# HGRN's levels inside 32 tokens as 32x32 products, their copy on ScalarE, and the LRU's convolution a step ahead of its gates

## The chip, the cores and the metric

One Trainium2 chip, one of its cores. The metric is the device time of one execution in microseconds (us). A core has a matrix engine (TensorE, PE in the profile, its weight loads PEld), VectorE (DVE), ScalarE (ACT), GpSimd (POOL) and a queue engine (SyncE, SP). Each runs its own list of instructions in order, and they meet at semaphores. Matrix results go to PSUM, eight banks of 512 fp32 columns by 128 partitions, here the tensor P.

## The reference

Two blocks follow each other over 512 tokens of width 1024. The change lies in the second block, in its hybrid mixer, which runs once in each of two layers on 16 meta tokens and 512 tokens (T = 528):

```python
proj = jnp.einsum('btd,dc->btc', h, w_in)
hq, hf, hi, hg, rq, rk, rv, rg, lx, ly = jnp.split(proj, IN_SPLITS, axis=-1)
# HGRN, four heads of 128: S_t = diag(f_t) S_{t-1} + k_t^T v_t ;  o_t = S_t^T q_t
o_hg = merge_heads(rmsnorm(hgrn2_chunked(q, k, v, log_f), hg_norm_g)) * jax.nn.silu(hg)
# retention, four heads: rope(rq), rope(rk), fixed decay per head
# LRU: a causal convolution of width 4, then two gates, then a scan
xc = causal_dwconv(lx, lru_conv_w, lru_conv_b)
o_lru = rg_lru(xc, gate_a_w, gate_a_b, gate_i_w, gate_i_b, lru_lambda) * jax.nn.gelu(ly)
return jnp.einsum('btc,cd->btd', jnp.concatenate([o_hg, o_ret, o_lru], -1), w_out)
```

The decay of HGRN differs for each channel and token, so the scores inside a block of 128 tokens, sum over d of q_t * decay(t, s) * k_s, can't be had from one product. The kernel builds them by levels: at level lev the pairs (s, t) that lie in the two halves of a block of 2^(lev+1) tokens get their decay as a factor on q times a factor on k.

## The kernel before

Every large product is done as three fp32r matmuls of high and low parts (L486, and L528 for the tiles with tokens on the partitions). The weights come by DMA into `raw`; ScalarE rounds them to `WH` (L1052), VectorE makes `WL` (L1508). A mixer runs over 20 tiles of projections (`MIXER_TILES`); a tile has 8 slots of 6 matmul records of 264 columns, a wide one 20.

The rest of the mixer is cut into steps that are woven between these slots. Each of TensorE, ScalarE and VectorE has its own version of every thread (`hgrn`, `lru`, `ret_scores`, `ret_values`, `lru_gate`), a generator that yields at the end of a step, and `mixer_threads` fixes for all three the same number of steps and the slots between which they fall due: a thread with n steps between slots s0 and s1 has done (slot - s0) * n // (s1 - s0) of them. Threads due at the same slot go in the order in which they are listed. HGRN's four heads have 13 steps each, head 1 between slots 46 and 90, the LRU 6 steps between 52 and 82, the retention's scores 5 between 70 and 104. Evictions of tiles and WH stand at a tile's end on ScalarE, WL two slots into the next tile on VectorE.

A head of HGRN: in step 1 VectorE makes A and K (hA, hK; L1860, L1862) and the operands of level 0; in steps 2 to 7, levels -1 to 4, TensorE multiplies for each of the four blocks of 128 tokens kb by qa, 128x128, into bank 4 (L812; an fp32 matmul is two records), and below level 4 the 16x16 piece of the meta tokens into bank 5 (L816). VectorE then copies what the level's mask lets through into `SM` (L1880) and into `SC`, 128x512 (`merge`, L1854), and prepares QA, KB, B and A two levels on (`prep`, L1837 to L1850). TensorE's next level waits for the merge, since it writes the same bank. Step 8 has levels 5 and 6 as 64-wide and 32-wide products (L825, L830) and the last merge on VectorE. Step 9 transposes KB into KT (ScalarE copies it, L1288), step 10 makes the state products, step 11 the output from SC, VI, S and QA (L858 to L864), step 12 the norm.

The LRU has two halves n of 128 channels, three steps each: convolution on VectorE (L1926, three L1929) and gate a on TensorE (L492 with gw) in the first, gate i, ScalarE's sigmoids, tanh and exp (L1315 to L1321) and VectorE's L1933 to L1938 in the second, square root (L1324), L1941 and the scan (L1943) in the third.

## Time and profile before

| | us |
|---|---|
| median of three runs | 2834.41 |
| the three runs | 2832.61 to 2837.95 |
| the profiled execution | 2833.47 |
| its span | 2831.4 |
| mean granted clock of TensorE | 0.979 |

The span runs from the first to the last instruction of the profiled execution; about 2 us lie around it. The two mixers take the stretches from about 1388 to 1640 and from 2118 to 2370 us of the span. In a timeline row "x8" is eight records merged, the first number is the start, the second the length from the first start to the last end; brackets give the idle time of that engine before the row and what ended it. A line such as L492 can be a helper's: there the names of the tiles tell the place.

### The profile page before, as it was taken

The page shows a single profiled execution, that of the slowest core. Times are in us where ns is not written, and L with a number is a line of the kernel's source. Part 1 is how long each engine was busy: PE and PEld are TensorE (multiplying, and loading weights), DVE is VectorE, ACT ScalarE, POOL GpSimd, SP SyncE. Part 2 cuts the span into 40 slices and gives each one's busy share as a digit, 9 for nine tenths or more (in the row PEclk, how much of TensorE's full clock was granted, in tenths as well). Part 3 has the DMA queues.
Part 4 walks back from the last instruction along what each step waited for, and adds up shares of the span by engine and source line. Part 5 has one row for each costly group of instructions (what it writes and reads, how often), then busy time and mean ns, then how long its engine had stood idle before and what let it go on. Part 6 is the DMA issues. An engine that isn't in the chain of part 4 may idle for free.

```text
span 2831.4 us, 39106 instructions
## 1 busy us (share of the span) xinstructions
PE 2671.2 (94%) x17256; PEld 2349.0 (83%) x17256; DVE 1366.2 (48%) x2039; ACT 1037.7 (37%) x1565; POOL 30.8 (1%) x69
## 2 busy tenths in 40 slices
PE   7999999998999899999879989999988899899998
PEld 5776788886776688887778889999988798899998
DVE  4766433334566543333556445554235653555532
ACT  3554422214445432222433344443233334444421
POOL 0000000000000000000000000000000000000000
PEclk9999999999999999999899999999999999999999
DMA  4222222222121222222211122222231012222221
GB/s 167 87 64 75 75 89 95 93 95 89 67 84 59 76 90 104 88 95 86 83 60 45 50 102 75 90 90 96 85 125 60 31 61 91 75 90 90 88 96 71
DMA packets 38425, 235.82 MB, mean 83 GB/s; under 512 B 5248, under 2 KB 5248, under 8 KB 15984
## 3 DMA queue, kind: packets, MB, share of 16 engines
q1 hardware_dynamic: 33312, 213.93, 21.5%
q0 software_dynamic: 3792, 17.30, 1.7%
q8 instruction: 135, 2.21, 0.3%
q10 hardware_dynamic: 1152, 2.10, 0.2%
q14 instruction: 34, 0.28, 0.0%
HBM read 222.69 MB, written 6.42 MB: 81 GB/s over the span
## 4 chain that ended last, share of the span: by engine, by line
PE 85%; DVE 8%; ACT 6%; issue 1%; DMA 1%; ACTq 0%; DVEq 0%
PE P L486 71%; PE P L492 3%; PE P L528 2%; PE P L550 2%; DVE WL L1508 1%; PE P L812 1%; ACT WH L1052 1%; PE P L743 1%; PE P L562 1%; PE P L576 1%; PE P L605 1%; DVE X L1716 1%; DVE small L1719 0%; DMA X<-in_xT 0%; PE P L719 0%
## 5 line engine op out<-in xcount | busy, mean ns | idle before, releaser
L486 PE MATMUL P<-XH,WL 128*128 128x264 f32 (+1 forms) x3008 | 826.5, 330 | 62.6 <-DVE WL L1508 30.0
L486 PE MATMUL P<-XL,WH 128*128 128x264 f32 (+1 forms) x3008 | 805.4, 323 | 0.0
L486 PE MATMUL P<-XH,WH 128*128 128x264 f32 (+1 forms) x3008 | 802.9, 323 | 0.0
L1508 DVE TENSOR_TENSOR WL<-raw,WH 128x1024 fp32r<-128x1024 f32 (+1 forms) x404 | 483.7, 1201 | 554.7 <-ACT WH L1052 554.3
L1052 ACT ACTIVATE WH<-raw 128x1024 fp32r<-128x1024 f32 (+1 forms) x404 | 417.8, 1038 | 668.7 <-PE P L486 664.8
L486 PEld LDWEIGHTS P<-XH,WL 128*128 128x128 f32 x3008 | 509.0, 191 | 115.8 <-issue 23.8
L486 PEld LDWEIGHTS P<-XH,WH 128*128 128x128 f32 x3008 | 505.2, 191 | 42.3
L486 PEld LDWEIGHTS P<-XL,WH 128*128 128x128 f32 x3008 | 506.5, 191 | 38.1
L2046 DVE SCALAR_TENSOR_TENSOR tmp<-P,PP,tmp 128x527 f32<-128x527 f32 x88 | 67.5, 767 | 223.4 <-ACT tmp L1453 223.4
L1453 ACT ACTIVATE tmp<-P,PP 128x528 f32<-128x528 f32 x88 | 69.6, 791 | 216.7 <-PE P L486 216.7
L486 PE MATMUL P<-GHH,WL 128*128 128x264 f32 x704 | 142.6, 284 | 0.0
L486 PE MATMUL P<-GHH,WH 128*128 128x264 f32 x704 | 142.4, 283 | 0.0
L486 PE MATMUL P<-GHL,WH 128*128 128x264 f32 x704 | 142.3, 283 | 0.0
L486 PE MATMUL P<-HH,WL 128*128 128x512 f32 x352 | 139.2, 396 | 0.0
L486 PE MATMUL P<-HL,WH 128*128 128x512 f32 x352 | 139.2, 396 | 0.0
L486 PE MATMUL P<-HH,WH 128*128 128x512 f32 x352 | 139.2, 395 | 0.0
L486 PEld LDWEIGHTS P<-GHL,WH 128*128 128x128 f32 x704 | 109.1, 188 | 0.0
L486 PEld LDWEIGHTS P<-GHH,WL 128*128 128x128 f32 x704 | 108.9, 188 | 0.0
L486 PEld LDWEIGHTS P<-GHH,WH 128*128 128x128 f32 x704 | 108.5, 188 | 0.0
L1171 ACT ACTIVATE tmp<-P 128x512 f32<-128x512 f32 x44 | 26.3, 598 | 166.5 <-PE P L486 166.5
L1648 DVE TENSOR_TENSOR tmp<-tmp,P 128x512 f32<-128x512 f32 x44 | 30.3, 688 | 108.1 <-PE P L486 108.1
L486 PEld LDWEIGHTS P<-HH,WL 128*128 128x128 f32 x352 | 66.2, 188 | 16.0
(325 smaller groups left out, 3491.5 us busy)
## 6 DMA issues: line engine op xcount, KB each, us to landing
raw<-in_wts SPq DMA_DIRECT2D x170, 1024.0 KB, 4.8
raw<-in_wts SPq DMA_DIRECT2D x32, 896.0 KB, 4.5
spill<-X POOLq DMA_DIRECT2D x2, 2112.0 KB, 6.9
X<-spill POOLq DMA_DIRECT2D x16, 264.0 KB, 3.7
tmp<-in_biasT POOLq DMA_DIRECT2D x16, 256.0 KB, 4.3
qswap<-qraw SPq DMA_DIRECT2D x44, 64.0 KB, 2.0
tab<-in_tR POOLq DMA_DIRECT2D x2, 1056.0 KB, 5.6
X<-in_xT ACTq DMA_DIRECT2D x8, 256.0 KB, 12.9
```

Of the source, the lines that this page charges most:

```text
L486: ins = nc.tensor.matmul(P[:, a:a + x1 - x0], wb[:, s, 128 * k:128 * k + 128], xb[:, kx, x0 - c0:x1 - c0], start=start and i == 0, stop=st ...
L492: ins = nc.tensor.matmul(P[:, a:a + x1 - x0], m, src[:, x0 - c0:x1 - c0], start=start, stop=stop)
L528: ins = nc.tensor.matmul(o, xb[:, k, c0:c1], wb[:, (u + k // 4) % NS, 256 * (k % 4):256 * (k % 4) + 256], start=n == 0 and k == 0 and i == ...
L550: ins = nc.tensor.matmul(o, xb[:, k, c0:c1], wb[:, (u + k // 4) % NS, 256 * (k % 4):256 * (k % 4) + 256], start=n == 0 and k == 0 and i == ...
L562: ins = nc.tensor.transpose(P[:, 512 * b + 128 * j:512 * b + 128 * j + 128], src[:, 128 * j:128 * j + 128], ident)
L576: nc.tensor.matmul(P[:, o:o + ke], q[64 * m:64 * m + 64, lane, 128 * i:128 * i + 128], k[64 * m:64 * m + 64, 2 + lane, 0:ke], start=(j == ...
L605: ins = nc.tensor.matmul(P[:, o + 128 * j:o + 512], VN[:, j, vc:vc + 128], aTs[lane][:, 512 * j:384 * j + 512], start=(j == 0), stop=(j == 3))
L1052: nc.scalar.activation(WH[:, u % NS, 0:length(u)], raw[:, u // 2 % RAW, a:a + length(u)], ACT.Copy).then_inc(*act.up("whi", u))
L1453: nc.scalar.activation(y[:, :], pair_bank(n % 4), ACT.Identity, bias=par("fcb", 44 * l + c), scale=PP[:, k:k + 1]).then_inc(*act.up("tap", ...
L1508: nc.vector.tensor_tensor(WL[:, u % NS, 0:length(u)], raw[:, u // 2 % RAW, a:a + length(u)], WH[:, u % NS, 0:length(u)].bitcast(F), ALU.su ...
L1648: nc.vector.tensor_tensor(t, t, bank(n % 4), ALU.mult).then_inc(*dve.up("mul", l, m))
L2046: nc.vector.scalar_tensor_tensor(y[:, 1:T], p[:, 0:T - 1], w(1), y[:, 1:T], ALU.mult, ALU.add).then_inc(*dve.up("conv1", l, n))
```

## The change

HGRN. For levels -1 to 4, whose pairs all lie within 32 tokens, TensorE makes only the sixteen 32x32 products on the diagonal, four for each of the blocks, into a compact area of bank 4: rows r to r+32 and columns 32 j to 32 j + 32. The piece for the meta tokens goes into columns 128 to 144 of the same bank. VectorE merges both with one masked copy of 144 columns (128 at level 4) into the new tile `SD`; `SM` and the copy of its own go. The masks have 6 levels of 144 columns instead of 8 of 128. In step 8 ScalarE copies the four row groups of SD to their places in SC, waits for levels 5 and 6, and copies three areas of bank 4 (two 32 x 4x32, one 64 x 4x64) into SC; VectorE's last merge goes. The state product, which needs bank 4, waits for ScalarE's last copy.

LRU. It has 8 steps instead of 6, between slots 52 and 86: the convolution is in a half's first step, gate a in the second, gate i in the third, the scan in the fourth. The retention's scores move by 4 slots, to 74 to 108.

```diff
@@ mixer_threads
-                   (lru(), 6, 52, 82), (ret_scores(), 5, 70, 104), (ret_values(), 9, 157, 193), (lru_gate(), 3, 190, 204))
+                   (lru(), 8, 52, 86), (ret_scores(), 5, 74, 108), (ret_values(), 9, 157, 193), (lru_gate(), 3, 190, 204))
@@ pe_program, hgrn
                     for j in range(4):
-                        c = META + 128 * j
-                        ins = nc.tensor.matmul(P[:, 2048 + 128 * j:2048 + 128 * j + 128], kb[:, c:c + 128], qa[:, c:c + 128],
-                                               start=(j == 0), stop=(j == 3), skip_group_check=True)
+                        for r in range(0, 128, 32):
+                            c, o = META + 128 * j + r, 2048 + 32 * j
+                            ins = nc.tensor.matmul(P[r:r + 32, o:o + 32], kb[:, c:c + 32], qa[:, c:c + 32],
+                                                   start=(j == 0), stop=(j == 3), skip_group_check=True)
                     if lev < 4:
-                        take(5)
-                        ins = nc.tensor.matmul(P[0:16, 2560:2576], kb[:, 0:16], qa[:, 0:16], start=True, stop=True)
-                        give((5,), ("hm", l, h, lev))
+                        ins = nc.tensor.matmul(P[0:16, 2176:2192], kb[:, 0:16], qa[:, 0:16], start=False, stop=True,
+                                               skip_group_check=True)
@@
-                give((4,), ("hc", l, h, 6))
+                give((4,), ("hsc", l, h))
@@
-                pe.wait_ge(*at("hc", l, h, 6))
+                pe.wait_ge(*at("hsc", l, h))
+                pe.wait_ge(*at("hd1", l, h, 7))
@@ pe_program, lru
                 for n in range(2):
+                    yield
                     pe.wait_ge(*at("lconv", l, n))
@@ act_program, hgrn
-                for _ in range(8):
-                    yield
+                for _ in range(7):
+                    yield
+                act.wait_ge(*at("hc", l, h, 4))
+                if h:
+                    act.wait_ge(*at("hpv", l, h - 1))
+                else:
+                    act.wait_ge(*at("hz1", l))
+                for r in range(0, 128, 32):
+                    nc.scalar.activation(scd[r:r + 32, :, r:r + 32], SD[r:r + 32, 0:128].rearrange("p (j c) -> p j c", c=32), ACT.Copy
+                                         ).then_inc(*act.up("hsd", l, h, r))
+                act.wait_ge(*at("hs", l, h, 6))
+                pb = bank(4).rearrange("p (j c) -> p j c", c=128)
+                for i, (r0, r1, c) in enumerate(((0, 32, 32), (64, 96, 96), (0, 64, 64))):
+                    nc.scalar.activation(scd[r0:r1, :, c:c + r1 - r0], pb[r0:r1, :, c:c + r1 - r0], ACT.Copy
+                                         ).then_inc(*act.up(*(("hsc", l, h) if i == 2 else ("hs6", l, h, i))))
+                yield
@@ act_program, lru
                 for n in range(2):
+                    yield
                     act.wait_ge(*at("lga", l, n))
@@ dve_program, hgrn
                 def merge(lev):
-                    mk = masks[:, lev + 1, :].unsqueeze(1).broadcast_to([128, 4, 128])
-                    nc.vector.copy_predicated(scd, mk, bank(4).rearrange("p (j c) -> p j c", c=128)).then_inc(*dve.up("hc", l, h, lev))
+                    n = 144 if lev < 4 else 128
+                    nc.vector.copy_predicated(SD[:, 0:n], masks[:, lev + 1, 0:n], P[:, 2048:2048 + n]).then_inc(*dve.up("hc", l, h, lev))
@@
-                    if lev < 4:
-                        nc.vector.copy_predicated(SM[:, :], masks[0:16, lev + 1, 0:16], P[0:16, 2560:2576]).then_inc(*dve.up("hm", l, h, lev))
@@
-                dve.wait_ge(*at("hc", l, h, 4))
-                merge(6)
@@ dve_program, lru (behind the convolution's yield)
+                    yield
                     yield
                     dve.wait_ge(*at("lsi", l, n))
```

The order on the engines moves at three places. On TensorE, layer 0, between head 1's level 0 and level 1 (L492 with gw is the LRU's gate a, first half; x2 are the two column ranges of a tile):

```order
+L486 MATMUL P<-XH,WH 128x264 x2
+L813 MATMUL P<-hQA,hKB 32x32 x16
+L816 MATMUL P<-hQA,hKB 16x16
+L486 MATMUL P<-XH,WL 128x264 x2
+L486 MATMUL P<-XL,WH 128x264 x2
+L486 MATMUL P<-XH,WH 128x264 x2
 L492 MATMUL P<-X,gw 128x264 x2
```

Gate a stood directly behind level 0; now three slots, level 1 and one more slot stand ahead of it. On VectorE the same place, from the WL two slots into the tile of lx1 to behind the convolution, before:

```order
L1508 TENSOR_TENSOR WL<-raw,WH 128x1024 [waits act_done]
L1880 COPY_PREDICATED SM<-masks,P 16x16 [waits pe_done]
L1854 COPY_PREDICATED SC<-masks,P 128x512
L1839 TENSOR_TENSOR hQA<-hQ,hA 128x66x4 [waits dve_done]
L1841 TENSOR_TENSOR hKB<-hK,hB 128x528
L1847 TENSOR_TENSOR hB<-hB,hA 128x66x4 [waits dve_done]
L1850 TENSOR_TENSOR hA<-hA 128x66x4 [waits dve_done]
L1926 TENSOR_SCALAR X<-X,PP 128x528
L1929 SCALAR_TENSOR_TENSOR X<-X,PP 128x528 [waits dve_done] x3
```

and now:

```order
L1525 TENSOR_TENSOR WL<-raw,WH 128x1024 [waits act_done]
L1871 COPY_PREDICATED SD<-masks,P 128x144 [waits pe_done]
L1856 TENSOR_TENSOR hQA<-hQ,hA 128x66x4 [waits dve_done]
L1858 TENSOR_TENSOR hKB<-hK,hB 128x528
L1864 TENSOR_TENSOR hB<-hB,hA 128x66x4 [waits dve_done]
L1867 TENSOR_TENSOR hA<-hA 128x66x4 [waits dve_done]
L1940 TENSOR_SCALAR X<-X,PP 128x528
L1943 SCALAR_TENSOR_TENSOR X<-X,PP 128x528 [waits dve_done] x3
```

The convolution keeps its place behind level 2's operands; one masked copy stands where two stood. On ScalarE, the LRU's second half, from the sigmoid of gate i on, before (L1295, L1296: head 1's output; L1374, L1375: the tile hf2):

```order
L1318 ACTIVATE X<-P,PP 128x528 [waits pe_done]
L1320 ACTIVATE tmp<-X,lbv 128x528 [waits act_done]
L1321 ACT_TABLE_LOAD
L1321 ACTIVATE X<-X,lbv 128x528
L1324 ACT_TABLE_LOAD
L1324 ACTIVATE tmp<-tmp 128x528 [waits dve_done]
L1295 ACTIVATE tmp<-P 128x528 [waits pe_done]
L1296 ACTIVATE hQA<-P 128x528
```

and now:

```order
L1335 ACTIVATE X<-P,PP 128x528 [waits pe_done]
L1337 ACTIVATE tmp<-X,lbv 128x528 [waits act_done]
L1338 ACT_TABLE_LOAD
L1338 ACTIVATE X<-X,lbv 128x528
L1311 ACTIVATE tmp<-P 128x528 [waits pe_done]
L1312 ACTIVATE hQA<-P 128x528
L1391 ACT_TABLE_LOAD
L1391 ACTIVATE tmp<-P 128x528
L1392 ACTIVATE tmp<-P 128x528
L1054 ACTIVATE WH<-raw 128x1024
L1341 ACT_TABLE_LOAD
L1341 ACTIVATE tmp<-tmp 128x528 [waits dve_done]
```

The square root (L1324, now L1341) has moved behind head 1's output, the eviction of hf2 and a WH.

## Rows read from the trace of the kernel before

**Rows 1.** The page's part 1: busy time, share of the span, instructions.
```profile
PE 2671.2 (94%) x17256; PEld 2349.0 (83%) x17256; DVE 1366.2 (48%) x2039; ACT 1037.7 (37%) x1565; POOL 30.8 (1%) x69
```

**Rows 2.** TensorE's waits in layer 0's mixer: total us, times, longest.
```profile
PE P L492 <- DVE X L1929: 11.6, 2, 5.8
PE P L812 <- DVE hK L1862: 2.3, 2, 1.6
...
PE P L812 <- DVE SC L1854: 2.0, 1, 2.0
PE P L492 <- ACT hQA L1296: 1.2, 1, 1.2
PE P L858 <- DVE S L1899: 1.1, 1, 1.1
PE P L492 <- ACT X L1318: 0.8, 1, 0.8
```

**Rows 3.** Timeline, TensorE: start, length, line, form, count, [idle before].
```profile
1454.50 2.13 PE L492 MATMUL P<-X,gw 128*128 128x264 f32 x4 [5.75 <-DVE X L1929]
...
1460.13 1.05 PE L812 MATMUL P<-hQA,hKB 128*128 128x128 f32 x8
...
1482.60 2.13 PE L492 MATMUL P<-X,gw 128*128 128x264 f32 x4 [5.83 <-DVE X L1929]
```

**Rows 4.** Busy time by stretch; after POOL comes the granted clock.
```profile
1454.50:1458.00 3.50, 3.50 (x12) 3.09 (x13) 0.00 (x0) 0.70 (x1) 0.00 (x0) 0.50 0.02 5
1470.00:1476.00 6.00, 5.25 (x44) 5.12 (x45) 5.83 (x13) 1.56 (x2) 0.00 (x0) 1.00 0.00 0
```

**Rows 5.** Chain that ended last, 1380 to 1600: start, us, what.
```profile
1506.59 2.19 PE P L486 x18
1508.78 0.90 PE P L492 x4
1509.70 1.28 ACT L1299
```

**Rows 6.** Timeline of TensorE, head 0's products of three widths.
```profile
1410.17 1.05 PE L812 MATMUL P<-hQA,hKB 128*128 128x128 f32 x8
...
1411.30 0.51 PE L486 MATMUL P<-XH,WL 128*128 128x264 f32 x2
...
1417.16 0.41 PE L486 MATMUL P<-XH,WH 128*128 128x264 f32 x2
1417.50 0.68 PE L825 MATMUL P<-hQA,hKB 128*64 128x64 f32 x8
1418.11 0.45 PE L830 MATMUL P<-hQA,hKB 128*32 128x32 f32 x16
1418.48 0.51 PE L486 MATMUL P<-XH,WL 128*128 128x264 f32 x2
```

**Rows 7.** Groups by form, VectorE, 1388 to 1640: busy, mean ns | idle before.
```profile
L1854 DVE COPY_PREDICATED SC<-masks,P 128x512 f32<-128x512 uint8 x28 | 20.2, 722 | 0.7 <-PE P L812 0.7
...
L1880 DVE COPY_PREDICATED SM<-masks,P 16x16 f32<-16x16 uint8 x20 | 3.2, 161 | 19.6 <-PE P L816 19.6
```

**Rows 8.** Timeline of VectorE, head 1's first levels and the convolution.
```profile
1444.92 0.15 DVE L1880 COPY_PREDICATED SM<-masks,P 16x16 f32<-16x16 uint8 x1
...
1445.62 0.68 DVE L1837 TENSOR_TENSOR hQA<-hQ,hA 128x528 f32<-128x528 f32 x1
...
1452.07 2.38 DVE L1929 SCALAR_TENSOR_TENSOR X<-X,PP 128x528 f32<-128x528 f32 x3
```

**Rows 9.** Groups by form, ScalarE, 1388 to 1640.
```profile
L1288 ACT ACTIVATE KT<-P 128x384 f32<-128x384 f32 x4 | 2.0, 489 | 6.2 <-PE P L839 6.2
...
L1289 ACT ACTIVATE KT<-P 16x128 f32<-16x128 f32 x4 | 1.0, 249 | 0.0
```

**Rows 10.** Timeline of ScalarE, the LRU's second half.
```profile
1496.93 0.64 ACT L1324 ACTIVATE tmp<-tmp 128x528 f32<-128x528 f32 x1 [0.22 <-DVE tmp L1938]
...
1507.69 1.06 ACT L1052 ACTIVATE WH<-raw 128x1024 fp32r<-128x1024 f32 x1
```

28 lines of the change are left out of this document (15 added, 13 removed).

## The prediction

> **What bounds the kernel now.** I read the page first. TensorE is busy for 94% of the span [rows 1], so whatever VectorE and ScalarE do only counts where TensorE stands still for it or where it adds to TensorE's own work. The change touches the two mixers alone, so the next view is the list of waits in the first mixer: the reader should see that two waits of L492 (the LRU's gate matmul) for L1929 (its convolution on VectorE) make 11.6 us, 2.3 us go to hK, which this change leaves alone, and the next ones are 2.0 us for VectorE's merge (L1854), 1.2, 1.1 and 0.8 us [rows 2]. Without hK that is 16.7 us. The second mixer has the same code. Then the timeline: both gate waits are nearly equal, 5.75 and 5.83 us, and what follows them is slow: from 1454.50 to 1460.13, 5.63 us, TensorE does four records of L492 and three slots of L486 [rows 3], which elsewhere take 0.90 and 2.19 us in the chain [rows 5]. The stretch behind the first wait has a granted clock of 0.50, that is 1.2 instead of 2.4 GHz; the stretch that holds the 1.97 us wait keeps 1.00 [rows 4]. So a wait of 5.8 us costs another 5.63 - 3.09 = 2.5 us, and one of 2 us none. Per layer, waits and clock are 16.7 + 5.0 = 21.7 us.
>
> **Part 1: the convolution a step ahead.** A slot of TensorE's main work is 2.19 / 3 = 0.73 us [rows 5]. Before, convolution and gate a stand at the same slot, 57, so TensorE arrives at 1454.50 - 5.75 = 1448.75 and waits until the convolution ends (1452.07 + 2.38 = 1454.45) [rows 3, 8]. Now gate a stands at slot 61: four slots, 2.9 us, and head 1's level 1 (about 0.9 us) later, at about 1452.6. The convolution itself comes earlier by two merges (part 2, 0.47 us each), at about 1453.5. That leaves a wait of about 1.2 us with the restart, where there were 5.75. I then carried this walk on with the same durations (each instruction's start to the next one's on its engine), in the new order:
> - Level 4 waited 1.97 us for a merge behind the LRU's second step. That step still waits for ScalarE's two sigmoids, tanh, table load and exp, but begins earlier against TensorE: about 0.3 us is left. The next product (level 6) now finds its operands behind the scan: 0.9 us.
> - The second gate a stands at slot 78, its convolution in VectorE's step at slot 74, behind the last hKB and hQA products. TensorE needs 4 x 0.73 + 0.3 = 3.2 us from one to the other. VectorE has the rest of a level, two products like hQA's 0.68 and the convolution's 0.6 + 2.38 [rows 8], 5 us: a wait of about 1.8 us, where there were 5.83.
> - The retention's first permutation is now issued ahead of the second gate i, which needs the same banks: 0.7 us in place of the 0.8 for L1318. The 1.1 us for S and the 1.2 us for hQA (ScalarE's copy) go, since those producers now have over 3 us.
> - What is late next: the square root of the LRU's second half. Before, it followed the exp on ScalarE. Now it is queued behind head 1's two output evictions, the eviction of hf2 with its table load and a WH: about 1.1 + 1.3 + 1.0 + 1.0 us, and a table load of 1.28 more [rows 5, 10]. VectorE sits at L1956 meanwhile, and behind that are the scan, a WL, head 1's normalisation and the second rotation, for which TensorE's score matmul of the retention (L903's place, slot 95) waits: by the walk about 3.1 us. Before, it did not wait.
> Returned are 1.2 + 0.3 + 0.9 + 1.8 + 0.7 + 3.1 = 8.0 us, and for the clock, since 3.1 us lies between 1.97 (no drop) and 5.75 (drop), half of 2.5: 9.3 us. Net 21.7 - 9.3 = 12.4 us a layer, **25 us** for both. The bounds: nothing returned, 43 us; twice the returns, 6 us.
>
> **Part 2: merges into a compact area.** On VectorE a merge of 512 columns takes 722 ns and the small one 161 ns [rows 7]; between 16 and 512 elements that is 1.13 ns an element, so 144 elements take about 0.31 us. In pitch: small and large merge together hold VectorE from 1444.92 to 1445.62, 0.70 us [rows 8]; one of 144 holds it some 0.23. A head saves 5 x 0.47 + 0.4 for level 4 + 0.6 for the merge that goes: 3.4 us of VectorE, 27 us over eight heads. Only where TensorE waits for VectorE is that time, and there it is in the walk above; for the other heads TensorE waits for hK and for little else [rows 2]. ScalarE gets seven copies a head: six of 128 elements, by the 249 ns of the 16x128 copy, and one of 256, between 249 and 489 [rows 9]: 1.9 us a head, 15 us in all, on an engine that is 37% busy [rows 1]. Copy needs no table load where L1288 had none. What is queued behind them is one eviction (rk1 for head 1, hg2 for head 2, rg0 for head 3) and the copy into KT for which the state product of step 10 waits. In the walk KT is ready 0.25 us ahead of head 1's state product: hidden, but barely.
>
> **Part 3: TensorE's own products.** Each level goes from 8 records of 128x128 to 32 of 128x32. Before, a level with its 16x16 product runs from 1410.17 to 1411.30, 1.13 us; the shape that now comes, L830, does 16 records from 1418.11 to 1418.48, 23 ns each [rows 6]. Thirty-two are 0.74 us, and the 16x16 product 0.15: 0.89. Going from L486 to the narrower shape took 0.34 us (1417.16 to 1417.50) where a pair of L486 takes 2.19 / 9 = 0.24: 0.10 more [rows 5, 6]. So a level saves 1.13 - 0.99 = 0.14 us, and the forty with the small product 5.6; the eight last ones about nothing. I take **5 us**. The bounds: L830 alternates between two groups of output partitions, the new loop goes round four. If four run as two did at half the price per record, 0.37 us less a level, 18 us more gain. If they ran like L825, all in one group, 0.61 us for 8 or 76 ns each [rows 6], a level would cost 32 x 0.053 = 1.7 us more, 81 us in all. I stay at 23 ns because L830 has the very shape.
> The Trainium skill, "TensorEngine Tiling (Array Packing)", Key Properties, says that changing the tiling mode drains TensorE: by that rule 48 levels each pay twice, and the trace agrees in kind, with the 0.10 us above. "TensorE: Matmul & The Clock Gate", Wait — 56ns, not 53.3ns?, states that start to start never falls below about 25 ns; by that figure the 32 records would be 0.80 us (an estimate), the gain of this part 2 us, and the sum 2807 for 2804. The row has 23 ns and decides.
>
> **The sum.** Against the profiled execution, 2833.5 us (span 2831.4): 2833.5 - 25 - 5 = 2803.5. It stands 0.9 us under the median of the three runs, so I give **2804 us**.
>
> **The rivals.**
> - A, the waits just go: ScalarE's late square root costs nothing, or the four groups are cheaper. 2834 - 43 - 5 = 2786. For it: half of the returns hang on one long chain of mine. Against: VectorE has 3 to 5 us of queued work at each of those places.
> - B, the wait moves to ScalarE or VectorE: ScalarE's step 8 waits for TensorE and VectorE in turn with an eviction and KT behind it. If each of eight heads pays 1.5 us at its state product, or the retention waits twice as long and the clock falls with it, 8 x 1.5 = 12 us come back: 2816, up to 2826. For it: the margin of 0.25 us. Against: ScalarE is 37% busy [rows 1], and its wait in step 8 is for things that are done one slot before the eviction behind it.
> - C, slower: the 32x32 products do not overlap. From 23 ns to p they cost 48 x 32 x (p - 23) ns; the 30 us are used up at p = 43 ns. At L825's 76 ns the time is 2834 - 25 + 81 = 2890. For it: no row shows 32 such records in a row, nor groups 32 and 96. Against: 16 records at 23 ns, entry and exit included.
> - D, no change: the LRU stays late because VectorE as a whole is behind, and each wait appears again one level later: 2834. For it: no row of VectorE between 1444.92 and the convolution has an idle before it [rows 8]. Against: the convolution needs 3 us, which the four slots give it.
> Chances: forecast 0.62, A 0.13, B 0.14, C 0.07, D 0.04. The range of 8 in 10 leaves out C, D and the better part of A: 2788 to 2826. 0.2% (5.7 us, about what a measurement tells from no change) is reached by the forecast, A and B: faster 0.89, same 0.04, slower 0.07.
>
> **What would show it.** In the profile after: the waits of L492 for the convolution (L1943 there) at 1 to 2 us each instead of 5.8, and a granted clock of 1.00 behind them (part 1); a new wait before the retention's first score matmul of about 3 us for its rotation; the merges at about 0.31 us, VectorE's busy time down by about 30 us, ScalarE's up by about 15; TensorE with 12 x 2 x 48 = 1152 more matmul records, a level from its first record to the next L486 in 0.9 us. I am wrong if a level takes over 1.8 us (C), if the state product waits for KT (B), or if L492 still waits over 4 us (D).

## The result, and the profile of the changed kernel

The changed kernel takes **2788.13 us** (median of five runs, 2782.37 to 2789.82), the kernel before 2832.99 us in the same series. The ratio is 0.9838, with a 95% interval of 0.9822 to 0.9854: a gain of 45 us (46 by the ratio), where I had forecast 30. The profiled execution has a span of 2785.3 us, 46.1 less than before.

The page's part 1, changed kernel; its row of before is [rows 1]:

```profile
PE 2640.8 (95%) x18408; PEld 2319.1 (83%) x18408; DVE 1339.2 (48%) x1991; ACT 1055.2 (38%) x1621; POOL 30.7 (1%) x69
```

TensorE has 18408 - 17256 = 1152 more matmuls, as the change demands, and yet is busy 30.4 us less. VectorE is busy 27.0 us less (forecast "about 30 us") and ScalarE 17.5 us more ("about 15").

TensorE's waits in the first mixer, changed kernel (total us, times, longest), against [rows 2]:

```profile
PE P L492 <- DVE X L1943: 3.9, 2, 2.5
PE P L905 <- DVE X L1987: 3.3, 1, 3.3
PE P L813 <- DVE hK L1879: 1.6, 1, 1.6
PE P L813 <- DVE SD L1871: 1.0, 1, 1.0
PE P L825 <- DVE hKB L1860: 0.9, 1, 0.9
PE P L492 <- DVE X L1985: 0.7, 1, 0.7
```

The two gate waits shrank from 11.6 to 3.9 us. The merge's wait is 1.0 instead of 2.0 us, and those for hQA, S and L1318 are gone. New are 3.3 us before the retention's score matmul (L905, formerly L903's place), 0.9 us before the level-6 products (L825) and 0.7 us for L1985. Without hK that is 9.8 us where there were 16.7; the second mixer reads alike.

The timeline of TensorE at the three largest (start, length, line, form, count, [idle before]), against [rows 3], and the granted clock behind the first and the third (the number after the busy time), against [rows 4]:

```profile
1451.32 2.13 PE L492 MATMUL P<-X,gw 128*128 128x264 f32 x4 [2.55 <-DVE X L1943]
...
1475.39 1.16 PE L492 MATMUL P<-X,gw 128*128 128x264 f32 x4 [1.40 <-DVE X L1943]
...
1500.75 0.22 PE L905 MATMUL P<-X 32*16 32x16 f32 x4 [3.34 <-DVE X L1987]
```

```profile
1451.40:1454.50 3.10, 3.10 (x10) 0.50 0.03 5
1500.80:1504.00 3.20, 3.20 (x29) 0.66 0.23 90
```

The first gate has a granted clock of 0.50 behind it, 1.2 instead of 2.4 GHz, and its four records take 2.13 us, exactly as before the change. The second, after 1.40 us of waiting, has its four records in 1.16 us, at the full clock. Behind the score matmul the clock is low too, 0.66 over 3.2 us.

What had shrunk most are TensorE's own products. Two levels of head 0 in the changed kernel (the first with the 16x16 product, the second, level 4, without it), against [rows 6]; then, in the kernel before, the L486 ahead of the level of [rows 6], and level 4:

```profile
1408.58 0.40 PE L486 MATMUL P<-XH,WH 128*128 128x264 f32 x2
1408.92 0.46 PE L813 MATMUL P<-hQA,hKB 128*32 128x32 f32 x32
1409.19 0.20 PE L816 MATMUL P<-hQA,hKB 128*16 128x16 f32 x2
1409.33 0.51 PE L486 MATMUL P<-XH,WL 128*128 128x264 f32 x2
...
1412.44 0.46 PE L813 MATMUL P<-hQA,hKB 128*32 128x32 f32 x32
1412.83 0.52 PE L486 MATMUL P<-XH,WL 128*128 128x264 f32 x2
```

```profile
1409.93 0.40 PE L486 MATMUL P<-XH,WH 128*128 128x264 f32 x2
...
1414.33 1.05 PE L812 MATMUL P<-hQA,hKB 128*128 128x128 f32 x8
1415.13 0.49 PE L486 MATMUL P<-XH,WL 128*128 128x264 f32 x2
```

A level with the small product now takes 1409.33 - 1408.92 = 0.41 us to the next L486, where 1.13 us stood in [rows 6]. Level 4 takes 0.39 us instead of 0.80. The 32 records start within 0.27 us, 8.5 ns each on the average. The way into a level got longer: from the last pair of L486 to the level's first record it is 1408.92 - 1408.58 = 0.34 us, where it was 1410.17 - 1409.93 = 0.24. So a level with the small product costs TensorE 0.72 - 0.10 = 0.62 us less, and level 4 0.31 us less.

The merges and copies by form (busy, mean ns | idle before), changed kernel, against [rows 7, 9], and VectorE's timeline at head 1's first level and the convolution, against [rows 8]:

```profile
L1871 DVE COPY_PREDICATED SD<-masks,P 128x144 f32<-128x144 uint8 x20 | 6.4, 318 | 11.2 <-PE P L816 11.2
```

```profile
L1293 ACT ACTIVATE SC<-SD 32x128 f32<-32x128 f32 x16 | 4.9, 306 | 5.7 <-DVE SD L1871 5.4
...
L1298 ACT ACTIVATE SC<-P 32x128 f32<-32x128 f32 x8 | 2.1, 268 | 1.8 <-PE P L830 1.6
...
L1298 ACT ACTIVATE SC<-P 64x256 f32<-64x256 f32 x4 | 1.5, 378 | 0.1
```

```profile
1442.66 0.32 DVE L1871 COPY_PREDICATED SD<-masks,P 128x144 f32<-128x144 uint8 x1
1442.88 0.70 DVE L1854 TENSOR_TENSOR hQA<-hQ,hA 128x528 f32<-128x528 f32 x1
...
1448.89 2.38 DVE L1943 SCALAR_TENSOR_TENSOR X<-X,PP 128x528 f32<-128x528 f32 x3
```

A merge is 318 ns (forecast 0.31 us) and holds VectorE for 0.22 us until the next instruction starts (forecast 0.23). The small copies on ScalarE are 306 and 268 ns, where I had taken 249. The convolution ends at 1448.89 + 2.38 = 1451.27; it ended at 1454.45 before. Most of these 3.2 us are not VectorE's: head 1 as a whole begins 2.26 us earlier (the part on the prediction has the rows).

### The profile page after: what moved, and what is told of

It reads as the page before. It is cut to its first block, busy times and chain, and to the rows that moved or that the text cites. A ratio compares the mean times of both kernels' runs of the same rounds, so it can differ in the third digit from the quotient of the medians.

```text
span 2785.3 us, 41408 instructions
## 1 busy us (share of the span) xinstructions
PE 2640.8 (95%) x18408; PEld 2319.1 (83%) x18408; DVE 1339.2 (48%) x1991; ACT 1055.2 (38%) x1621; POOL 30.7 (1%) x69
## 3 DMA queue, kind: packets, MB, share of 16 engines
q10 hardware_dynamic: 1152, 2.10, 0.2%
## 4 chain that ended last, share of the span: by engine, by line
PE 86%; DVE 7%; ACT 6%; DMA 1%; issue 1%; SPq 0%; ACTq 0%; DVEq 0%
PE P L486 72%; PE P L528 3%; PE P L492 3%; PE P L550 2%; DVE WL L1525 1%; ACT WH L1054 1%; PE P L743 1%; PE P L562 1%; PE P L576 1%; PE P L605 1%; PE P L813 1%; DVE X L1733 1%; DVE small L1736 1%; DMA X<-in_xT 0%; PE P L719 0%
## 5 line engine op out<-in xcount | busy, mean ns | idle before, releaser
L486 PE MATMUL P<-XH,WL 128*128 128x264 f32 (+1 forms) x3008 | 826.9, 330 | 62.6 <-DVE WL L1525 30.0
L486 PE MATMUL P<-XL,WH 128*128 128x264 f32 (+1 forms) x3008 | 805.4, 323 | 0.0
L486 PE MATMUL P<-XH,WH 128*128 128x264 f32 (+1 forms) x3008 | 802.5, 322 | 0.0
L486 PEld LDWEIGHTS P<-XH,WL 128*128 128x128 f32 x3008 | 508.0, 191 | 115.7 <-issue 23.8
L486 PEld LDWEIGHTS P<-XH,WH 128*128 128x128 f32 x3008 | 504.4, 191 | 42.0
L486 PEld LDWEIGHTS P<-XL,WH 128*128 128x128 f32 x3008 | 505.9, 191 | 38.0
L486 PE MATMUL P<-GHH,WL 128*128 128x264 f32 x704 | 142.9, 284 | 0.0
L486 PE MATMUL P<-GHH,WH 128*128 128x264 f32 x704 | 142.6, 283 | 0.0
L486 PE MATMUL P<-GHL,WH 128*128 128x264 f32 x704 | 142.4, 284 | 0.0
L486 PE MATMUL P<-HH,WL 128*128 128x512 f32 x352 | 139.4, 396 | 0.0
L486 PE MATMUL P<-HL,WH 128*128 128x512 f32 x352 | 139.4, 396 | 0.0
L486 PE MATMUL P<-HH,WH 128*128 128x512 f32 x352 | 139.4, 396 | 0.0
L486 PEld LDWEIGHTS P<-GHL,WH 128*128 128x128 f32 x704 | 109.0, 188 | 0.0
L486 PEld LDWEIGHTS P<-GHH,WL 128*128 128x128 f32 x704 | 108.9, 188 | 0.0
L486 PEld LDWEIGHTS P<-GHH,WH 128*128 128x128 f32 x704 | 108.6, 188 | 0.0
L486 PEld LDWEIGHTS P<-HH,WH 128*128 128x128 f32 x352 | 66.3, 188 | 15.8
```

The source lines that it names most:

```text
L486: ins = nc.tensor.matmul(P[:, a:a + x1 - x0], wb[:, s, 128 * k:128 * k + 128], xb[:, kx, x0 - c0:x1 - c0], start=start and i == 0, stop=st ...
```

## The experiments

In the order of what they answer. Every kernel was timed against the kernel before on the same chip; the gain is (1 - ratio) x 2833 us. The intervals are about 4 to 6 us wide to either side, so differences of a few us between two kernels are read from the traces: the last two columns give stretches of TensorE's timeline, in us, for the first and the second mixer. "Head 0" runs from the first record of head 0's level -1 to that of head 1; the LRU has no part in it, so it prices six levels. "Heads 1, 2" runs on from there to head 3's level -1 and holds the LRU and the retention's scores.

| kernel | ratio | 95% | gain, us | head 0 | heads 1, 2 |
|---|---|---|---|---|---|
| the kernel before | 1 | | | 47.8, 47.8 | 126.9, 127.0 |
| changed kernel | 0.9838 | 0.9822 to 0.9854 | 46 | 44.4, 44.4 | 111.8, 111.8 |
| LRU part alone | 0.9899 | 0.9885 to 0.9914 | 29 | 47.9, 47.8 | 115.4, 115.3 |
| products alone | 0.9924 | 0.9909 to 0.9938 | 22 | 44.5, 44.6 | 123.0, 123.1 |
| products and compact merges, no LRU part | 0.9902 | 0.9885 to 0.9918 | 28 | 44.4, 44.4 | 120.3, 119.7 |
| products and LRU part, old merges | 0.9867 | 0.9846 to 0.9887 | 38 | 44.7, 44.6 | 115.5, 118.9 |
| products over one column group at a time | 0.9871 | 0.9856 to 0.9886 | 37 | 46.8, 46.8 | 112.1, 112.0 |
| products over two groups at a time | 0.9840 | 0.9825 to 0.9854 | 45 | 45.0, 45.0 | 111.4, 112.8 |
| products issued twice | 0.9853 | 0.9836 to 0.9869 | 42 | 46.0, 46.0 | 111.2, 111.2 |
| changed kernel, early square root | 0.9811 | 0.9795 to 0.9828 | 54 | 44.3, 44.4 | 109.4, 109.7 |
| convolution two steps ahead | 0.9865 | 0.9849 to 0.9882 | 38 | 44.4, 44.4 | 115.6, 115.6 |
| both of these | 0.9867 | 0.9853 to 0.9882 | 38 | 44.4, 44.4 | 116.0, 116.0 |
| early square root, LRU steps over 40 slots | 0.9881 | 0.9864 to 0.9898 | 34 | 44.4, 44.4 | 118.2, 118.5 |
| early square root, TensorE's LRU one slot later | 0.9789 | 0.9775 to 0.9802 | 60 | 44.4, 44.4 | 107.8, 107.8 |

### The parts one at a time

**The LRU part alone**, on the kernel before:

```diff
-                   (lru(), 6, 52, 82), (ret_scores(), 5, 70, 104), ...
+                   (lru(), 8, 52, 86), (ret_scores(), 5, 74, 108), ...
 # and one more yield in lru() on TensorE (ahead of gate a), on ScalarE, and on VectorE (behind the convolution)
```

> The kernel before with the LRU's part alone (8 steps from 52 to 86, the convolution a step ahead of gate a, the retention's scores at 74 to 108); HGRN as before. Theory P (the products were priced too high, the rest of the prediction holds): the gate waits fall from 5.8 us to about 3.5 and 2.3, longer than in the changed kernel since two large merges stand ahead of each convolution; with the new wait of 3.3 us at the retention's scores and one half-clock stretch, 15 to 19 us of gain, about 2816. Rival V (the gain missing from the prediction came from VectorE's shorter merges): the LRU's part needs them, alone it gives under 10 us, 2823 or more.

It gained 29 us, more than either side gave it: theory P had the two gate waits at 3.5 and 2.3 us and a stretch at half clock. TensorE's timeline at its three waits, and the clock behind the second:

```profile
1454.15 1.16 PE L492 MATMUL P<-X,gw 128*128 128x264 f32 x4 [1.39 <-DVE X L1931]
...
1477.40 1.16 PE L492 MATMUL P<-X,gw 128*128 128x264 f32 x4 [2.05 <-DVE X L1931]
...
1502.79 0.22 PE L904 MATMUL P<-X 32*16 32x16 f32 x4 [3.33 <-DVE X L1975]
```

```profile
1477.40:1481.00 3.60, 3.60 (x23) 1.00 0.00 0
```

The waits are shorter, and shorter together than the changed kernel's, since TensorE with its old, longer levels gets to the gates later: at the first one 9.8 us after the start of head 1's level -1 where the changed kernel has 7.8, while the convolution ends after 11.2 us against 10.3. Here no gate wait lowers the clock: after 1.39 and after 2.05 us the gate's four records take 1.16 us, and the clock is 1.00. The 3.33 us before the score matmul is there as in the changed kernel, so it belongs to the LRU part, not to ScalarE's new copies.

**The changed kernel without the LRU part**: the diff above taken out again.

> The changed kernel without the LRU's part (6 steps from 52 to 82, the retention's scores at 70 to 104). Theory P: 40 levels each 0.6 us and 8 levels 0.3 us shorter on TensorE, 27 us, and the four gate waits of 5.8 us each shorter by up to 0.9 us where that isn't eaten by TensorE arriving earlier: 2803 to 2808. Rival V: the same total of 25 to 30 us, but with the products at 5 us and the rest in shorter waits. Both theories give about 2805 here; what tells them apart is where the trace has it, and the next kernel.

**The products alone**, on the kernel before: 32x32 products, written to the diagonal of the old area, the old merges behind them.

```diff
-                        c = META + 128 * j
-                        ins = nc.tensor.matmul(P[:, 2048 + 128 * j:2048 + 128 * j + 128], kb[:, c:c + 128], qa[:, c:c + 128],
+                        for r in range(0, 128, 32):
+                            c, o = META + 128 * j + r, 2048 + 128 * j + r
+                            ins = nc.tensor.matmul(P[r:r + 32, o:o + 32], kb[:, c:c + 32], qa[:, c:c + 32],
 # start and stop as before
```

> The kernel before with the 32x32 products alone: they are written to the diagonal of the same 128x512 area, and VectorE merges it as before, in 0.72 us, with the small merge of its own; the last merge stays on VectorE; the LRU as before. Theory P: TensorE's levels alone give 24 to 27 us, less what waits for VectorE take back, about 2810; a level from its first record to the next L486 takes 0.41 us in place of 1.13. Rival V: 5 us, 2828.

Products alone gained 22 us, and with the compact merges 28. TensorE's wait at the gates in the first mixer with the compact merges, and then with the products alone:

```profile
PE P L492 <- DVE X L1941: 10.9, 2, 6.3
```

```profile
PE P L492 <- DVE X L1930: 12.8, 2, 7.2
```

Against [rows 2], where the gate waits are 11.6 us, the compact kernel's are 10.9 in the first mixer (and 12.4 in the second). They grew to 12.8 us in either mixer with the products alone (the longest 7.2), and the merge's wait from 2.0 to 2.6. TensorE gets there earlier and VectorE does not. The stretches say the same: head 0 is 3.3 us shorter with the products alone, and heads 1 and 2, with twice as many levels, only 4.0 us. So the 22 us are what was left after the waits took some back.

**Products and LRU part, with the old merges**, which closes the square:

> The changed kernel without its compact area: 32x32 products written to the diagonal blocks of the old 128x512 area, the old merges on VectorE, and the LRU's new steps; it completes a square of four with the products alone (0.992), the LRU alone (0.990) and the changed kernel (0.984). Theory O (the parts overlap on TensorE: faster products bring it to the convolution's wait earlier, and what the compact merges give is VectorE's time there): the gain is less than the sum 21 + 28 = 49 us, about 36 to 40 us, ratio 0.986 to 0.987, and the waits for the convolution are longer than the changed kernel's 2.5 and 1.4 us. Rival I (the parts are independent, and the compact merges with ScalarE's spreading give nothing or cost): 49 us, ratio 0.983, as fast as the changed kernel or faster.

It gained 38 us, where 22 + 29 = 51 would be the sum: theory O. TensorE's wait at the gates, and the clock behind its second gate wait, which was 2.03 us long:

```profile
PE P L492 <- DVE X L1932: 5.3, 2, 3.3
```

```profile
1475.20:1479.00 3.80, 3.80 (x16) 0.62 0.00 0
```

The gate waits are 5.3 us here, 3.4 in total with the LRU part alone and 3.9 in the changed kernel. The compact merges are then worth 46 - 38 = 8 us on this side of the square and 28 - 22 = 6 us on the other. The intervals of each pair overlap by a little, so only the sum of the evidence (the same sign twice, and shorter waits) speaks for them, and their size is known to a few us at best. The trace of the kernel with the old merges shows how rough such a difference is: both its mixers have the same gate waits, and heads 1 and 2 take 115.5 us in the first and 118.9 in the second. What differs is how long the clock was low.

### What a 32x32 product costs

**One column group at a time**: the loops of the changed kernel change places.

```diff
-                    for j in range(4):
-                        for r in range(0, 128, 32):
+                    for r in range(0, 128, 32):
+                        for j in range(4):
```

> The changed kernel with the two loops round the 32x32 products exchanged: four products in a row go to the same 32 output partitions, instead of each to the next group. Same products, same number. Theory P (the four column groups run at the same time if neighbours in the order are in different groups): a level's 32 records take four times as long as 0.27 us or more, 1.1 to 2.4 us (the upper by the 76 ns of the 64-wide L825), so 40 to 100 us slower than the changed kernel, 2830 to 2890. A rival (the records are simply cheap, whatever their group): no difference, 2788.

**Two groups at a time**: the order of the groups is 0, 64, 0, 64 and so on, then 32, 96 and so on.

```diff
-                    for j in range(4):
-                        for r in range(0, 128, 32):
+                    for j, r in [(j, r) for rs in ((0, 64), (32, 96)) for j in range(4) for r in rs]:
+                        if True:
```

> The changed kernel with one edit: the 32x32 products of a level run over the column groups 0 and 64 first and over 32 and 96 after them, instead of over all four in turn. Four groups in turn took 0.27 us for the 32 records of a level (8.5 ns each), one group at a time about 21 ns each. Theory G (column groups work at the same time, so the time of a record falls with the number of groups that take turns): about 11 to 16 ns a record, a level of 0.45 to 0.6 us from first record to last, and a ratio to the kernel before some 0.001 to 0.002 above the changed kernel's 0.984, so 0.985 to 0.986. Rival N (what counts is that neighbouring records of one group stand apart by some minimum, and two groups are enough to hide it): 8.5 ns a record, 0.984. Rival S (only all four together are fast): 21 ns a record, as with one group, 0.987.

The same level of head 0 in TensorE's timeline, one group and then two:

```profile
1406.00 0.80 PE L813 MATMUL P<-hQA,hKB 128*32 128x32 f32 x29
...
1406.83 0.39 PE L528 MATMUL P<-WH,XL 128*128 128x256 f32 x1
```

```profile
1406.30 0.51 PE L813 MATMUL P<-hQA,hKB 128*32 128x32 f32 x26
...
1406.83 0.39 PE L528 MATMUL P<-WH,XL 128*128 128x256 f32 x1
```

To the next L528 a level takes 1406.83 - 1406.00 = 0.83 us with one group at a time and 1406.83 - 1406.30 = 0.53 with two, against the 0.41 with all four in turn. (The counts x29 and x26 are the merging of the view and not fewer products.)

Theory P's numbers for one group were far off: it had a level at 1.1 to 2.4 us and the time at 2830 to 2890, 40 to 100 us above the changed kernel, and the kernel lost 9. The starts of the single records in the traces tell why. In all three orders two records of the same group start 31 to 32 ns apart (52 ns for a group's second record), so a group's eight records need about 0.24 us. Records of different groups start as little as 6 ns apart. With four groups in turn all four run beside one another, and 0.24 us is nearly the whole level. And when the loop stays in one group, the next group's first record starts some 0.15 us after that of the group before it, long before that one is through: the groups overlap even then. So theory G holds in kind, the time of a level falls with the number of groups that run side by side, and "22 ns a record" in the one-group order (0.70 us over 32) is an average over overlapping groups and not the price of a record. The 76 ns a record of my rival C is far from all of this.

In time, one group cost 0.42 us x 48 = 20 us of TensorE's work (head 0 is 2.4 us longer, 19 us for eight heads), and the kernel lost 9 of them (46 to 37): TensorE comes later to its gates, waits 1.29 and 1.40 us there, and no low clock follows. That gave back about half. Two groups cost 0.12 x 48 = 6 us (head 0 is 0.6 us longer), of which the ratio shows nothing, and the trace has a reason for the first mixer. TensorE's first gate there and in the second mixer, two groups:

```profile
1455.39 1.16 PE L492 MATMUL P<-X,gw 128*128 128x264 f32 x4 [2.14 <-DVE X L1943]
...
2160.66 2.13 PE L492 MATMUL P<-X,gw 128*128 128x264 f32 x4 [2.14 <-DVE X L1943]
```

In the first mixer the clock stayed up behind the wait, and in the second, behind the same wait of 2.14 us in the same program, it fell.

**The products issued twice**:

```diff
-                    for j in range(4):
+                    for j in (0, 1, 2, 3, 0, 1, 2, 3):
```

> The changed kernel with each level's 32 products issued twice into the same places, 32 records more at each of 48 levels (6 levels, 4 heads, 2 layers). It prices a record by itself. Theory G (8.5 ns a record with four column groups in turn, mostly on TensorE's path): 48 times 0.27 is 13 us, less what falls into its waits for VectorE: 8 to 13 us over the changed kernel, ratio 0.987 to 0.989. Rival F (23 ns a record or more, as I had taken from the old level-6 products): 48 times 0.74 is 35 us, ratio 0.996. A rival by which most of a level is its entry and exit and records are free: under 3 us, 0.984.

TensorE's timeline, a level and the first gate:

```profile
1407.40 0.73 PE L813 MATMUL P<-hQA,hKB 128*32 128x32 f32 x62
...
1408.09 0.39 PE L528 MATMUL P<-WH,XL 128*128 128x256 f32 x1
...
1453.42 1.16 PE L492 MATMUL P<-X,gw 128*128 128x264 f32 x4 [1.68 <-DVE X L1943]
```

A level grew from 0.41 to 1408.09 - 1407.40 = 0.69 us, 0.28 us for 32 records: 8.8 ns each, on TensorE's path. The other 0.13 us of the 0.41 are the 16x16 product and the way out of the narrow shape, nearly all of it the way out, since level 4 without that product still takes 0.39; the way in, 0.10 us more than before, stands ahead of the first record and is not in the 0.41. The 32 records more are 13 us in all (head 0 is 1.6 us longer), but the time rose by only 4 us, or by 7 in the profiled executions; the intervals of the two kernels overlap. The gate row tells why it is less than 13: TensorE, later by its extra work, waits 1.68 instead of 2.55 us, and its records take 1.16 us instead of 2.13, since the clock stays up. Theory G gives the price of a record and not the loss: 6 to 9 of the 13 us came back, more than I had allowed for.

### What is left: three waits

**The square root with the exp** on ScalarE. In the changed kernel the timeline of ScalarE has the square root of the LRU's second half here, with its table load, as the prediction had placed it:

```profile
1492.20 1.28 ACT L1341 ACT_TABLE_LOAD   x1
```

```diff
                     nc.scalar.activation(la, la, ACT.Exp, scale=lbv[:, 26 + n:27 + n]).then_inc(*act.up("lea", l, n))
-                    yield
                     act.wait_ge(*at("la3", l, n))
                     nc.scalar.activation(tmp[3], tmp[3], ACT.Sqrt).then_inc(*act.up("lsq", l, n))
                     yield
+                    yield
```

> The changed kernel with one edit: ScalarE issues the LRU's square root in the same step as its exp, instead of one step later, behind other steps' work. Theory Q (the retention scores' wait of 3.3 us a layer, L905 on VectorE's L1987, comes from that late square root, which VectorE waits for with the scores' inputs queued behind it): the wait falls below 1.5 us in both layers, the stretch of low TensorE clock at 1498 to 1504 goes with it, and the kernel gains 3 to 7 us, ratio about 0.982. Rival V (VectorE is behind by its own work there): the wait stays above 2.5 us and the ratio is 0.984. Rival M (ScalarE now stands in the square root's wait while TensorE needs its evictions): new waits of TensorE on ScalarE of over 1 us, and 0.984 or more.

It gained 54 us, 8 more than the changed kernel. TensorE's wait at the score matmul in the first mixer with the clock behind it, and VectorE ahead of the retention's second rotation:

```profile
PE P L905 <- DVE X L1987: 2.3, 1, 2.3
```

```profile
1493.60:1497.00 3.40, 3.40 (x28) 0.60 0.02 5
```

```profile
1487.29 1.23 DVE L1525 TENSOR_TENSOR WL<-raw,WH 128x1024 fp32r<-128x1024 f32 x1 [2.37 <-ACT WH L1054]
1489.98 0.77 DVE L1919 SCALAR_TENSOR_TENSOR tmp<-hQA,PP,tmp 128x528 f32<-128x528 f32 x1 [1.47 <-ACT tmp L1318]
```

The wait fell from 3.3 to 2.3 us, not below 1.5, and the clock still falls behind it (0.60): theory Q names one cause of two. With the LRU's square root out of the way VectorE waits for ScalarE's WH (2.37 us) and for the exponential of head 1's normalisation (L1318, 1.47 us), which stand ahead of the rotation too. Two times 1.1 us do not make 8. In the trace heads 1 and 2 are 2.4 and 2.2 us shorter than the changed kernel's, so the mixers gained about 5 us; half of that is the waits, and the rest is in the main that the clock came back sooner behind the unchanged first gate wait, for which this edit gives no reason. What is beyond 5 us lies outside these stretches or in the intervals, which overlap: in the profiled executions the first mixer already begins 4.7 us earlier, ahead of anything that the edit touches.

**The convolution two steps ahead**, with 10 steps of the LRU over slots 52 to 92:

```diff
-                   (lru(), 8, 52, 86), (ret_scores(), 5, 74, 108), ...
+                   (lru(), 10, 52, 92), (ret_scores(), 5, 84, 114), ...
 # and one more yield in the same three places
```

> The changed kernel with the LRU's convolution two steps ahead of its gates instead of one: 10 steps of the LRU between slots 52 and 92 (before 8 between 52 and 86), the retention scores between 84 and 114 (before 74 and 108). Theory W (what is left of the convolution's wait, 2.5 and 1.4 us a layer, and the half clock behind the longer one are cost on TensorE's path): both waits go, the clock stays at its upper level behind the first gate, and the kernel gains 5 to 12 us, ratio 0.980 to 0.982. Rival R (VectorE is the late one whatever the order, and its lag is paid at the next thing that TensorE wants of it): the same 4 us come back as waits for the retention's inputs or for SD, and the ratio stays at 0.984.

> Both edits of the two runs before it: the square root with the exp, and the convolution two steps ahead. If theories Q and W both hold and their places are apart, the gains add: 8 to 19 us over the changed kernel, ratio 0.977 to 0.981. If the retimed LRU already moves the retention scores out of the square root's reach, it gives what the convolution two steps ahead gives alone. If VectorE is the late one whatever the order, 0.984.

Both gave 38 us, 8 less than the changed kernel. The intervals hardly overlap the changed kernel's, and the traces agree with the loss: heads 1 and 2 take 3.8 us more in each mixer. Two of TensorE's waits with the convolution two steps ahead:

```profile
PE P L847 <- ACT KT L1306: 3.0, 1, 3.0
...
PE P L813 <- DVE SD L1873: 2.1, 1, 2.1
```

Neither gate waits for its convolution any more, and none of it was gained: rival R. The state product now waits 3.0 us for KT (my rival B's place), and SD takes 2.1 us where it took 1.0; four more places have new waits of 1.0 to 1.7 us. The early square root changed nothing here, as the second case of its expectation had it.

**The LRU's 8 steps over 40 slots**, with the early square root:

```diff
-                   (lru(), 8, 52, 86), (ret_scores(), 5, 74, 108), ...
+                   (lru(), 8, 52, 92), (ret_scores(), 5, 79, 112), ...
```

> The changed kernel with the early square root (0.981) and the LRU's 8 steps spread over slots 52 to 92 (before 52 to 86), the retention scores between 79 and 112 (before 74 and 108), so that the gates stand one slot farther behind the convolution and not a whole step. Theory W2 (a little more distance takes the 2.6 us wait and the low clock behind it away, and the later steps are still done in time): the wait falls below 1.9 us, the clock stays up behind it, and the kernel gains 2 to 5 us on the early square root, ratio 0.979 to 0.980. Rival R (as with the convolution two steps ahead, the LRU's later work on VectorE and ScalarE runs into the third head's levels, and TensorE waits there for SD and KT): 0.982 to 0.986.

It gave 34 us, 20 less than the same kernel with 34 slots, and worse than either theory. The first half of W2 came true: the first gate's wait is 1.82 us, and its records take 1.16 us. What it cost stands later, in VectorE's timeline:

```profile
1488.23 0.71 DVE L1984 TENSOR_TENSOR X<-X,tab 128x528 f32<-128x528 f32 x1 [9.49 <-PE P L492]
...
1506.24 0.49 DVE L1879 TENSOR_SCALAR hK<-tmp,lbv 128x528 f32<-128x528 f32 x1
```

VectorE stands 9.49 us in the first rotation's wait for TensorE's permutation. Behind it are the LRU's second half down to the scan and the second rotation, and only then, at 1506.24, comes hK of head 2, for which TensorE waits 6.5 us. TensorE also waits 3.0 us for KT again. Six slots more decide here whether the LRU is through before the next head begins.

**TensorE alone one slot later**, with the early square root; VectorE and ScalarE keep their order:

```diff
-def mixer_threads(hgrn, lru, ret_scores, ret_values, lru_gate):
+def mixer_threads(hgrn, lru, ret_scores, ret_values, lru_gate, late=0):
-                   (lru(), 8, 52, 86), ...
+                   (lru(), 8, 52 + late, 86 + late), ...
 # TensorE's call passes late=1
```

> The changed kernel with the early square root (0.981), and on TensorE alone the LRU's steps one slot later (53 to 87); VectorE and ScalarE keep their order. Theory W3 (what harmed the retimed LRU was its later work on VectorE and ScalarE, not the gates' place on TensorE): each gate a waits 0.7 us less, 1.9 and 0.7 us instead of 2.6 and 1.4, the clock stays up behind the first, and the kernel gains 2 to 6 us on the early square root, ratio 0.979 to 0.9805. Rival L (VectorE and ScalarE now get the gates' results one slot later, and their lag is paid at the next level): the same time moves into waits for SD and hKB, 0.981 to 0.984.

**2775.91 us** (five runs, 2772.38 to 2779.31), ratio 0.9789: the fastest of all, with an interval apart from the changed kernel's. It overlaps that of the kernel with the early square root alone, from which it differs by the one slot; there the traces speak for it, with heads 1 and 2 shorter by 1.6 and 1.9 us. TensorE's waits, and the clock behind the first gate:

```profile
PE P L492 <- DVE X L1943: 2.5, 2, 1.8
...
PE P L813 <- DVE SD L1871: 1.7, 1, 1.7
...
PE P L847 <- ACT KT L1305: 0.4, 1, 0.4
```

```profile
1453.40:1457.00 3.60, 3.60 (x55) 1.00 0.02 5
```

The two gate waits are 1.8 and 0.7 us, as theory W3 said, and the clock behind the first is 1.00. A part came back as rival L had it, 0.7 us for SD and 0.4 for KT. So over the early square root alone the waits are only 0.6 us less, and the larger part of what it gained is the clock. What sets this retiming apart from the harmful ones is that nothing of VectorE's or ScalarE's order moved. That this is the reason is theory W3's reading; no run moves VectorE or ScalarE alone.

## Why the prediction was right or wrong

**Right in sign and in where to look, wrong in size**: 2788 stands at the low end of the range. The sum had two terms, 25 for the LRU part with the merges' help, and 5 for TensorE's products. The trace gives other figures for both.

**Part 3, TensorE's products: the step that failed.** "I take 5 us" should have been 40 x 0.62 + 8 x 0.31 = 27 us of TensorE's own work; the head 0 stretch, 3.4 us shorter, gives the same for eight heads. Three things went wrong in it, and one was right: the 0.10 us for the entry.
- I divided L830's 0.37 us by 16 to get 23 ns, though this time runs to the next L486 and so holds what it costs to leave the narrow shape. In the trace of before L830's sixteen records start within 0.25 us, 16 ns each, in two groups of 32 ns a record; 0.12 us are the way out. The price was there to be read.
- L830 alternates between two groups and the new loop goes round four. I named that, and kept it as a bound ("0.37 us less a level, 18 us more gain"), but took the price of two as the likeliest. With the entry a level came to 0.51 us where I had 0.99. The records with the way out took 0.39 where I had 0.74, which is that bound; the rest is the 16x16 product, which I had at 0.15 us and which adds 0.02.
- "The eight last ones about nothing": level 4 went from 0.80 to 0.39 us, 0.31 less with the entry. I had no row of it in the sum.

The page on the clock gate of the Trainium skill ("TensorE: Matmul & The Clock Gate", Wait — 56ns, not 53.3ns?), by which start to start never falls below about 25 ns, does not hold for these records: 8.5 ns in the changed kernel, 8.8 ns in the doubled one. Within one column group the trace stays above that figure, with 31 to 32 ns. By that page's figure the forecast would have been farther off still. The page "TensorEngine Tiling (Array Packing)" of the Trainium skill, Key Properties, by which a change of tiling mode drains TensorE, agrees in kind with what is left of a level: 0.10 us more on the way in, and 0.13 us behind the last of the 32 records, the small product among them.

**Part 1, the walk.** Point by point, forecast and measured, per layer in us:

| wait | forecast | changed kernel |
|---|---|---|
| first gate a | 1.2 | 2.55 |
| level 4 (SD) | 0.3 | 1.0 |
| level 6 | 0.9 | 0.9 |
| second gate a | 1.8 | 1.40 |
| gate i behind the permutation | 0.7 | 0.7 |
| score matmul | 3.1 | 3.3 |
| lost to the clock | 1.25 | about 4.5 |

For the clock: behind the first gate, four records of L492, two slots of L486, a level and two pairs of L486 more run from 1451.32 to 1457.58, 6.3 us, where the same work at the full clock takes 3.5 us, so 2.8 us; behind the score matmul the windows from 1498 to 1510 miss 1.7 us at full clock. The returns are 14.4 instead of 9.3 us, and the net 21.7 - 14.4 = 7.3 us a layer, 15 us instead of 25. The stretches give a little more: heads 1 and 2 are 15.1 us shorter, of which two heads' products are 6.8, so 8.3 us a layer or 17. With 27 for the products that is 42 to 44 us, against 46 in the spans: one term was too high by about 9, the other too low by 22, and 2 to 4 us stay open.

The first gate's error is part 3's error again. Head 1's level -1, where TensorE waits for hK in both kernels, gives both engines a common start; first before, then the changed kernel:

```profile
1443.28 1.16 PE L812 MATMUL P<-hQ,hK 128*128 128x128 f32 x8 [1.58 <-DVE hK L1862]
```

```profile
1441.02 0.46 PE L813 MATMUL P<-hQ,hK 128*32 128x32 f32 x32 [1.58 <-DVE hK L1879]
```

From there the convolution ends after 1451.27 - 1441.02 = 10.25 us, where it was 11.17: two shorter merges, 0.9 us, just as forecast. But TensorE is at the gate after 1451.32 - 2.55 - 1441.02 = 7.75 us, and the forecast had 1452.6 - 1443.28 = 9.3. The 1.6 us between them are three levels that each came cheaper than I had put them: the two ahead of the gate that were there before, at 0.62 us less, for which the walk took nothing off, and the one that joined them. The doubled products turn it round: with TensorE later, the wait is 1.68 us and the clock stays up. That the LRU part gives 29 us alone and 46 - 28 = 18 us on top of the rest is the same thing seen from the square.

The chain of the score matmul held, step for step: the square root's table load stands at 1492.20 behind the evictions and the WH, and the wait is 3.3 us. Its other half, head 1's normalisation, I had listed as queued there and not as a cause; with the early square root it is what VectorE waits for, together with WH.

**Part 2.** The merges' 0.31 us, their 0.23 us of pitch and VectorE's saving held. KT kept its margin: the changed kernel has no wait for it. The later retimings used that margin up, 3.0 us at once.

**The rivals.** A gave 2786, and the time is 2788, but that is luck: of its two reasons only one is true, "the four groups are cheaper", and its sum took 5 us for the products and all of the waits, 43 us, where the traces have 27 and about 16. The waits did not just go. B's mechanism is real and did not occur here; it is a part of what made the retimed kernels slower. C is refuted by the changed kernel and by one group at a time. D fell with the gate waits, although its idea, that a wait appears again later, is what the two-steps-ahead kernel did.

## What to carry to other kernels

Where a narrow product replaces a wide one, take the price of a record from start to start within its column group, keep entry and exit as a term of their own, and ask how many column groups run side by side; the loop order alone was worth 9 us here. When one part of a change makes the bounding engine faster, walk the waits of the other part again with that engine's new arrival time: a gain of 27 us on TensorE lengthened the very wait that the other part had shortened, and lost the clock with it. And to give a late producer time, move the consumer alone: one slot on TensorE gained in the one run that did it, while spreading the LRU over six more slots on every engine pushed the producer's later work in front of the next stage and lost 20 us.

## What the runs showed of the hardware

- **Records of 32x32 products in one column group start 31 to 32 ns apart, in different groups as little as 6 ns**, and groups overlap even when the loop visits them one after the other. Over four groups in turn that is 8.5 ns a record; over two a level takes 0.12 us more, over one 0.42 us more.
- **The clock after a wait is not a matter of the wait's length alone.** It stayed at 1.00 behind waits of 1.40, 1.68, 1.82 and 2.05 us, and fell to 0.50 behind 2.55 us. Behind 2.03 us in the kernel with the old merges it was 0.62, and behind 2.14 us in the kernel with two groups it stayed up in one mixer and fell in the other. What else decides, the runs do not tell.
- **Small copies on ScalarE go with the elements in a partition, on top of a fixed part.** Out of PSUM 128 elements in 32 partitions took 268 ns, 256 in 64 partitions 378 ns and 384 in 128 partitions 489 ns [rows 9]: 0.86 ns an element and about 158 ns (an estimate from these rows). Half the partitions changed little (16x128: 249 ns), and the same 32x128 out of SBUF took 306 ns.
